# A streaming encoder step on one Trainium2 core: three of eight gate chunks of the first pass made in the projection part, and small transfers issued by other engines

## The reference

```python
cq, ckv, kpe, bq, bk, bv, iq, iw, ik, ga, gb = jnp.split(h @ w_in, offs, axis=-1)
# mixer A: latent attention, 8 heads; mixer B: the 128 (sample: 72) best keys by the indexer, 8 heads
o_a = _query_blocks(mla_block, (qn, qp), q_chunk).reshape(Bn, T, A_HEADS * A_V)
o_b = _query_blocks(dsa_block, (bq, iq, iw), q_chunk).reshape(Bn, T, B_HEADS * B_HEAD_DIM)
merged = jax.nn.sigmoid(ga) * (o_a @ w_o_a) + jax.nn.sigmoid(gb) * (o_b @ w_o_b)
x = x + merged @ w_out
x = x + PEER(RMSNorm(x))   # 8 heads, 16 experts each of 128 x 128, their rows gathered by index
```

## Time and profile before

| | us |
|---|---|
| median of 3 runs | 1927.25 (1925.21 to 1929.27) |
| profiled execution | 1926.13 |
| its span, first to last instruction | 1924.3 |
| TensorE busy | 1298.7 (67%) |
| VectorE busy | 1325.8 (69%) |
| ScalarE busy | 575.3 (30%) |
| GpSimd busy | 522.0 (27%) |
| mean share of the DMA engines, slices 9 to 39 | about 0.9 and more |

### The profile page before, as it was taken

The page is one execution under the profiler, slowest core; times in us unless marked ns, Lnnn a source line. Parts: engine busy times, 40 slices in busy tenths (PEclk is TensorE's granted clock), DMA queues, the critical chain, the costliest instruction groups (busy, mean ns, idle before and its releaser), DMA issues.

```text
span 1924.3 us, 25838 instructions
## 1 busy us (share of the span) xinstructions
PE 1298.7 (67%) x8684; PEld 715.0 (37%) x8684; DVE 1325.8 (69%) x3948; ACT 575.3 (30%) x2040; POOL 522.0 (27%) x552
## 2 busy tenths in 40 slices
PE   7779884766887757577986766769877534444344
PEld 3447752234444432244553422446544211111111
DVE  3644228688886656789876666899866577686754
ACT  2223202342332222433431323324422222222222
POOL 0000003233332231333332323322322333333332
PEclk9878986967878878778888868778889755555555
DMA  5042348999999999999999999999999999999997
GB/s 205 6 135 78 122 151 334 414 423 426 425 423 424 400 413 418 409 425 425 367 425 422 423 424 391 423 425 351 384 424 422 425 426 426 427 426 424 427 422 313
DMA packets 121653, 704.92 MB, mean 366 GB/s; under 512 B 18224, under 2 KB 21344, under 8 KB 51376
## 3 DMA queue, kind: packets, MB, share of 16 engines
q0 software_dynamic: 78336, 570.46, 71.1%
q1 hardware_dynamic: 38672, 129.26, 17.5%
q10 hardware_dynamic: 4512, 3.54, 0.6%
HBM read 700.13 MB, written 3.02 MB: 365 GB/s over the span
## 4 chain that ended last, share of the span: by engine, by line
DMA 34%; DVE 21%; PE 21%; issue 16%; ACT 3%; POOL 1%; DVEq 0%; POOLq 0%
DMA rows<-in_peer_uv,index 25%; DVE rows L2043 9%; PE ps_v L1397 5%; DMA wch<-in_w_row 4%; PE ps_f L1104 2%; PE ps_f L1241 2%; DMA wch<-in_w_out 2%; PE ps_h L1377 2%; PE ps_f L1270 2%; DMA wch<-in_peer_wq 2%; PE ps_f L1291 1%; POOL rows L1081 1%; DMA wch<-in_keyb 1%; DVE score L1819 1%; PE ps_f L1256 1%
## 5 line engine op out<-in xcount | busy, mean ns | idle before, releaser
L1081 POOL DMA_INDIRECT rows<-in_peer_uv,index x544 | 520.2, 956 | 1285.9 <-PE ps_v L1397 1007.1
L2043 DVE CUSTOM_DVE_ANT_0 rows<-rows,ps_h 128x1024 f32<-128x1024 f32 x544 | 658.0, 1220 | 290.4 <-DMA rows<-in_peer_uv,index 217.0
L1397 PE MATMUL ps_v<-rows,diag 128*32 128x256 f32 x4352 | 431.9, 512 | 457.7 <-ACT diag L1651 440.9
L1397 PEld LDWEIGHTS ps_v<-rows,diag 128*32 128x32 f32 x4352 | 127.8, 133 | 711.2 <-ACT diag L1651 575.0
L1642 ACT ACTIVATE tan<-arg 128x2 f32<-128x2 f32 x272 | 55.5, 204 | 872.3 <-DVE arg L2053 838.5
L1645 ACT ACTIVATE weight<-tan,lead 128x1 f32<-128x1 f32 x544 | 180.8, 379 | 9.1
L1651 ACT ACTIVATE diag<-sel,weight 128x32 f32<-128x32 f32 x544 | 140.7, 305 | 0.0
L1241 PEld LDWEIGHTS ps_f<-bufh,wch 128*128 128x128 f32 x768 | 117.1, 239 | 22.7 <-issue 20.5
L1241 PE MATMUL ps_f<-bufh,wch 128*128 128x128 f32 x768 | 123.6, 328 | 0.0
L1104 PE MATMUL ps_f<-wch,bufh 128*128 128x512 f32 (+1 forms) x192 | 83.6, 574 | 30.6 <-DMA wch<-in_w_row 27.7
L1291 PE MATMUL ps_f<-bufh,wch 128*128 128x128 f32 x384 | 55.7, 305 | 11.7 <-DMA wch<-in_peer_wq 10.6
(11 more groups left out here) (319 smaller groups left out, 1740.4 us busy)
## 6 DMA issues: line engine op xcount, KB each, us to landing
wch<-in_w_gate SPq DMA_DIRECT2D x64, 512.0 KB
wch<-in_w_row SPq DMA_DIRECT2D x39, 512.0 KB
wch<-in_w_o SPq DMA_DIRECT2D x32, 512.0 KB
wch<-in_w_out SPq DMA_DIRECT2D x32, 512.0 KB
wch<-in_peer_wq SPq DMA_DIRECT2D x32, 512.0 KB
rows<-in_peer_uv,index POOLq DMA_INDIRECT x544
w_tok<-in_w_tok SPq DMA_DIRECT2D x4, 1640.0 KB, 13.6
wch<-in_keyb SPq DMA_DIRECT2D x6, 512.0 KB
```

The lines of the kernel that those rows point to most:

```text
L1081: pool.indirect_dma_start(rows[c % RING][:, :, :].rearrange("p a d -> p (a d)"), None, io.peer_uv[:, :], at).then_inc(s_uv[c % RING], 16)
L1397: ins = nc.tensor.matmul(ps_v[GROUP * a:GROUP * (a + 1), :], diag[:, c % DRING, :], rows[c % RING][:, 1, QD * a:QD * (a + 1)], start=False ...
L2043: v.tensor_tensor_reduce(out=u, in0=u, in1=ps_h[:, :], scale=1.0, scalar=0.0, op0=ALU.mult, op1=ALU.add, accum_out=dots[:, c % KEEP:c % KE ...
```

## The change

`SOON = 3`: chunks 0, 1 and 2 of the first pass are made in the projection part. Weights for their first three halves go to a place of their own (`m.soon`), loaded behind the other input of that part; those for the other three go over `w_tok` quarter 0 once TensorE has used it for tile 0. TensorE makes chunks 0 and 1 between `up` and the turning of the pairs, in the banks of `ps_x`, and chunk 2 between the pairs and the heads, in `ps_pj`; ScalarE takes the three tanh between the pairs' copies and the heads' copies. In the first pass of the stream part five chunks are left, 18 ticks each: halves at 6 and 12 of the 18, tanh at 13. The 16 copies into `vm` are issued by GpSimd, the two loads of `key0` by SyncE, behind the first four gate loads and the two loads of `xb`. Nothing is computed otherwise than before.

```diff
+SOON = 3
@@ project @@
+    later = w_tok[:, 0, :, :].rearrange("p c k -> p (c k)")[:, 0:SOON * D].rearrange(...)
+        def soon_at(j):
+            bank = ps_x[:, 4 * j:4 * j + 4, :].rearrange("p c k -> p (c k)") if j < 2 else ps_pj[:, j - 2, :]
+            return bank[:, 0:2 * (P + DEC)].rearrange("p (a k) -> p a k", a=2)
             sp.dma_start(x2[1][:, :], io.x_prompt[0:P, :]).then_inc(s_x[1], 16)
+            for n in range(SOON):
+                sp.dma_start(m.soon[:, n, :, :], io.w_gate[DC * (n % 2) + n // 2, :, :, :]).then_inc(s_soon, 16)
             for n, t in enumerate(FIRST):
+                if n:
+                    sp.wait_ge(s_proj, 4 * n + 1)
+                    for g in range(SOON, 2 * SOON):
+                        sp.dma_start(later[:, g - SOON, :, :], io.w_gate[...]).then_inc(s_later, 16)
                 sp.wait_ge(s_norm, n + 1)
@@ ScalarE @@
                 for g in range(3):
                     tr_out((t, "pair", g))
+                if following is None:
+                    for j in range(SOON):
+                        act.wait_ge(s_gate, j + 1)
+                        nc.scalar.activation(m.wide_sg[:, :, j, :], soon_at(j), ACT.Tanh, scale=0.5)
@@ TensorE @@
+            def gate(j):
+                if j >= 2:
+                    pe.wait_ge(s_pr, 4 * len(FIRST))
+                for a in range(2):
+                    n = 2 * j + a
+                    if n in (0, SOON):
+                        pe.wait_ge(s_later if n else s_soon, 16 * SOON)
+                    w = m.soon[:, n, :, :] if n < SOON else later[:, n - SOON, :, :]
+                    for k in range(DC):
+                        ins = nc.tensor.matmul(soon_at(j)[:, a, :], w[:, k, :], m.wide_h[:, k, 0:P + DEC], ...)
+                ins.then_inc(s_gate, 1)
                     projection(FIRST[n + 1])
+                else:
+                    for j in range(SOON - 1):
+                        gate(j)
                 for g in range(3):
                     turn((t, "pair", g))
+                if n + 1 == len(FIRST):
+                    gate(SOON - 1)
@@ stream @@
-        n = 6 * len(PASSES[p])
+        n = 6 if p else 18
-                    for n in range(WRING):
+                    for n in range(2 * SOON, 2 * SOON + WRING):
                         load_gate(p, n)
                     for i in members:
                         load_x(i)
+                    for r in range(2):
+                        sp.dma_start(key0[:, r, :], io.keyb[r, :, :]).then_inc(s_key0, 16)
@@ GpSimd @@
+            pool.wait_ge(s_zero, 1)
+            for h in range(H):
+                here, cols = slice(META * h, META * (h + 1)), slice(AV * h, AV * (h + 1))
+                pool.dma_start(vm[here, 0, cols], m.va_of(4)[DEC:DEC + META, h, :]).then_inc(s_vm, 16)
+                pool.dma_start(vm[here, 1, cols], m.vb_of(4)[DEC:DEC + META, :]).then_inc(s_vm, 16)
@@ ScalarE @@
-            act.wait_ge(s_zero, 1)
-            for h in range(H):
-                ...
-                act.dma_start(vm[here, 0, cols], m.va_of(4)[DEC:DEC + META, h, :]).then_inc(s_vm, 16)
-                act.dma_start(vm[here, 1, cols], m.vb_of(4)[DEC:DEC + META, :]).then_inc(s_vm, 16)
-            for r in range(2):
-                act.dma_start(key0[:, r, :], io.keyb[r, :, :]).then_inc(s_key0, 16)
```

37 lines of the change are left out of this document (26 added, 11 removed).

## The result

| | before | after |
|---|---|---|
| median of the runs, us | 1930.19 (1925.21 to 1932.47, 6 runs) | 1910.47 (1907.66 to 1919.1, 6 runs) |
| profiled execution, us | 1926.13 (span 1924.3) | 1911.97 (span 1910.2) |
| ratio, 95% interval | | 0.9907 [0.9883, 0.9932] |

By the ratio, which compares the means of the runs, the change takes 17.9 us off, with 13 to 23 us as the interval (the medians are 19.7 us apart). The forecast was 1903 us, with 23.6 us taken off the profiled execution. Measured twice more on other chips, the changed kernel came to 0.9915 [0.9885, 0.9946] and 0.9912 [0.989, 0.9934]. The three agree on some 17 us: the sign and most of the size were right, and the gain was forecast some 6 us too large.

The account below looks back on a forecast made before the run. Full DMA bounds the kernel from 302 us, so only time saved ahead counts, where TensorE is the bound from 109 to 218 us. -11.8 + 0.7 + 0.65 - 13.1 = -23.6 us gives 1903 us, range 1896 to 1912.

Parts of the forecast that it names:

- What bounds it: DMA is full from 302 us to the end; a microsecond saved ahead of the first gather moves everything later by one.
- ScalarE's transfers, -11.8: At the attention's start, without the small transfers on ScalarE, the first relu starts 11.8 us earlier.
- First gate's weights, +0.7: After the fourth score, the first gate waits for its weights: loss 0.7 us, between 0 and 4.
- Projection part, +0.65: Gate halves fill TensorE's wait for the pairs, but the part ends later: loss 0.65 us, between -0.5 and 3.
- Attention, first four stages: From the sample's index heads to the prompt tile's picked keys: gains of 0, 3.4, 2.1 and 1.7 us.
- Attention, last stage: From 194.06 to 217.95 us: gate halves leave, one stays, 23.9 us becomes 18.0, gain 5.9.
- Turning and blend: From the turning of the heads to the first output product: forecast change 0.
- Rival 1: Low clock in the attention's six-unit stretches makes second halves 2.2 us dearer, taking half its gain: 1910 us, chance 0.17.
- Rival 2: All freed gate halves come back in the attention, 19 us instead of 13.1: 1898 us, chance 0.10.
- Rival 3: The first gate waits for all four weight loads, 4 us instead of 0.7: 1907 us, chance 0.11.
- Rival 4: Slower than before: TensorE never leaves 1.2 GHz in the attention, +18 us: 1945 us, chance 0.03.
- Rival 5: No change: the earlier start is lost in the full DMA stretch, 1926 us, chance 0.04.

Follow-up runs that it names:

- e1_moves: The kernel before with only the 18 transfers moved off ScalarE, gate chunks left in the stream part: 1916.46 us, ratio 0.9933.
- e2_gates: The changed kernel with the 18 transfers back on ScalarE, so the gates' move alone: 1922.8 us, ratio 0.9962.
- t1_hidden: The changed kernel with eight of the ten gate halves where VectorE picks keys, none between ticks 26 and 66: 1909.48 us, ratio 0.9892.
- r2_before: The kernel before, unaltered, profiled again on another chip: 1926.11 us, ratio 0.9998.
- r1_after: The changed kernel, unaltered, profiled again on another chip: 1914.13 us, ratio 0.9915.
- b1_early: The kernel before with only its last pair of gate halves moved, from ticks 88 and 92 to 82 and 84: 1929.74 us, ratio 0.9983.
- f1_fill: t2_mixed with six idle matmuls, read by nobody, in the gaps of TensorE's last chain: 1907.93 us, ratio 0.986.
- e4_last: The changed kernel with only the last of its ten gate halves moved, from tick 84 to 91: 1911.56 us, ratio 0.9918.
- f2_hidden_fill: The changed kernel with halves at ticks 6, 12, 17, 20, 23, 26, 66, 72, 84, 92 and f1_fill's idle matmuls: 1907.93 us, ratio 0.9856.
- r4_more_fill: t2_mixed with 15 idle matmuls in the gaps of the last chain, measured again beside the unaltered changed kernel: 1906.01 us, ratio 0.9892.
- t2_mixed: The changed kernel with its ten gate halves at ticks 6, 12, 18, 24, 36, 48, 66, 74, 84, 92: 1904.99 us, ratio 0.9863.
- e3_late: The changed kernel with its ten gate halves at the ticks of the last ten before (40 to 92): 1916.33 us, ratio 0.9924.
- f4_hidden_fill: t1_hidden with 15 idle matmuls in the gaps of the last chain: 1898.57 us, ratio 0.9852.

## Why the forecast was right in sign and too large

- *What bounds it.* Right. The full DMA stretch moved as a block, and a gain ahead of it arrives one to one. (From the eighth slice on, have one below nine tenths, the last, and not two.)
- *ScalarE's transfers, -11.8.* Right. From TensorE's first score to the relu it is 0.68 us where before has 12.47 and 12.96, 11.8 and 12.3 less, and e1_moves alone is worth 12.3 by the medians. e2_gates' wait of 12.04 is the same wait as 11.80 in the earlier trace rows.
- *First gate's weights, +0.7.* Too small: the wait was 0.98, 1.04 and 2.37 us in the changed kernel, 1.5 in the mean. The stage grew by 0.3 only, because the half behind it took 3.9 to 4.1 us where before had 4.63; that the sum came out near 0.7 is luck.
- *Projection part, +0.65.* The sign was wrong, by 1.7 us in the change's favour. The distance from the up-projection to the key heads' turning fell from 17.87 to 17.48 us, since all the turnings ran at 2.4 GHz behind gate work (1.04 us where the earlier trace rows have 1.94 and 1.91), and by the end of ScalarE's last copy, from which the forecast counted, it fell from 20.27 to 19.22. This is a gain of 1.05, where the text had a loss of 0.65 and feared up to 3.
- *Attention, first four stages.* -3.5, -2.7, -1.6 against -3.4, -2.1, -1.7, and nothing in the index stage. The steps by VectorE's picking and by the halves hidden behind it (the first and third) hold to a tenth or two. The -2.7 is a mean of -3.7, -0.6 and -3.7, so that it lies near -2.1 is luck.
- *Attention, last stage: the step that failed.* "One stays and stands where TensorE waits for VectorE ...; then eight units with no gate, the last five at the low clock, some 0.3 us dearer each. 18.0." Measured 20.3 twice and 23.35 once. Three sizes in it were too small. A unit at the low clock is 1.60 us against 1.24 at the high one (185.52 - 184.28 in the changed kernel), 0.36 more. The early product behind the units doubles, 2.07 against 1.13, and was not in the sum. And the half is 2.44 or 4.35 us against a wait of 1.5, so it is not all hidden. In the two profiles with 20.3 these three come to some 0.3 + 0.9 + 0.9 = 2.1 of the 2.3 us missed; in the third the dear half adds 1.9 more. Without any half this stage takes 22.12 at the low clock (t1_hidden); before, less its two halves of 4.24 and 2.44, it took 17.2.
- *Turning and blend: the term that was missing.* The forecast shifted them as they were. They grew by 3.4 us from r2_before to r1_after: 0.8 from the turning to the blend (2.91 to 3.73) and 2.6 from there to the output product (18.69 to 21.28). The text had the low clock reach "the last five" units and then stopped asking how long it would last. The clock fell some 3 us behind the last half (in the changed kernel's first profile the half ends at 182.8, and 187 to 206 us are at 0.50) and stayed down through the turning into the blend. b1_early makes this cost out of the kernel before, f1_fill takes it away.
- *The rivals.* Rival 1 came nearest in number (1910) and in cause, the clock, but not in its mechanism: of the changed kernel's fifteen second halves in three profiles thirteen ran at 2.44 or less, and the loss is in the gateless end instead. Rival 2 (1898) did not happen. Rival 3 (weights): its wait of 4 us came in three variants (3.91 in e4_last, 3.89 in f2_hidden_fill, 3.96 in r4_more_fill), and the unaltered changed kernel had 2.37 at most. Rival 4 did not happen: the mean clock of the attention is 0.79, not 0.5. Rival 5 is refuted by the slope.

The last stage's 3.3 us and the tail's 3.5 are more than the whole miss; what the projection part, the transfers, the middle stage and the stretch ahead of the first gather gave beyond the forecast makes up for a part. The two steps that failed have one root: the low clock of the gateless end was priced for five units and no further.

## What to carry to other kernels

Work that is moved off an engine may have been what kept its clock up: after forecasting a gap or a gateless stretch, follow the low clock to the next long block of matmuls behind it and price that block too, since there it costs most (2.6 us in one blend). Put movable matmuls where another engine is late, and pay for the clock with a few idle matmuls in waits that exist anyway, just ahead of the long block; here 15 of them did it with no gate half near, the clock being back after the first six. And where the steps of one long engine program are judged from single profiles, count from an event close ahead: from the up-projection to the first gather two profiles of before agree to 0.01 us, though their absolute times differ by 3. Some of that is luck, since their stages differ by up to 0.5 us and cancel, and the changed kernel's three profiles spread from 200.86 to 205.20 by the same measure, so take more than one profile.

## What the runs showed of the hardware that was not expected

- The clock falls while TensorE never stands still. In t1_hidden from 137 to 151 us it is busy 14.00 of 14 us with small scores, turnings and value products, and has 0.50 throughout. The Trainium skill ("TensorE: Matmul & The Clock Gate", section "HAM oscillation — how this bites in real kernels") describes the fall as one that a gap between groups of matmuls brings; here there is no gap, and the clock is low all the same, so the Trainium skill's account does not cover this case. What decides it, no run here shows.
- With a few idle matmuls in gaps of 0.35 to 0.7 us TensorE keeps 2.4 GHz (f1_fill) where the same chain without them loses it (t2_mixed, e3_late; the kernel before keeps it without them). In f4_hidden_fill the clock is back from 1.2 GHz after six of them: the 2.4 GHz prices are there from 192.82 us on.
- With the same ticks and the same order, single gate halves are 2.44 us in one execution and 4 to 4.6 in the next, and so is the up-projection's first product (2.85 and 4.32 us in the two profiles of before). Such a draw moves a stage by 3 us and may be part of why runs of one kernel differ by 10 us; no run separates it.
- A copy of 16 rows took 0.48 us to issue on GpSimd, against 0.64 on ScalarE, half of what its gathers suggested.
- The full DMA stretch of one and the same kernel differs by up to 7 us between executions (1628.5 and 1621.4), with equal traffic (412 GB/s over 1628 us, 414 over 1621). What decides it stays open.
